# An RWKV-7 triangular inverse moved from two array quadrants to four

## The reference

```
S_t = S_{t-1} (diag(decay_t) - kk_t^T (kk_t * a_t)) + v_t^T k_t
o_t = S_t r_t
```

## Time and profile before

| | |
|---|---|
| median of 3 runs | 2339.93 us |
| the profiled execution | 2337.96 us |
| its span | 2336.3 us |
| TensorE busy (matmul) | 2150.9 us, 92% |
| VectorE busy | 912.5 us, 39% |
| ScalarE busy | 634.7 us, 27% |
| mean granted TensorE clock | 0.966 |

### The profile page before, as it was taken

How to read it: one execution, slowest core, us unless ns; L and a number is a source line. 1 busy time by engine, 2 the same in 40 slices (tenths; PEclk the granted TensorE clock), 3 DMA queues, 4 the chain that set the end, 5 groups by cost and what they waited for, 6 DMA issues and landing times. The chain is left out here.

```text
span 2336.3 us, 47109 instructions
## 1 busy us (share of the span) xinstructions
PE 2150.9 (92%) x20794; PEld 1409.6 (60%) x20794; DVE 912.5 (39%) x1765; ACT 634.7 (27%) x1433; POOL 319.8 (14%) x279
## 2 busy tenths in 40 slices
PE   7999999999999999997997999999898788489997
PEld 3577585675866857754554555556566555355664
DVE  3253462543634535323323313062321777522332
ACT  5321222223223223122214111132221566211111
POOL 0000020110201101020001032120010566101110
PEclk9999999999999999999999999999997999799998
DMA  7100010000100000007002022100002000556662
GB/s 255 30 20 11 10 41 19 29 21 10 31 26 27 17 19 30 21 15 281 1 27 104 27 85 76 54 10 9 28 27 73 1 1 1 201 172 225 209 194 92
DMA packets 52798, 147.84 MB, mean 63 GB/s; under 512 B 11459, under 2 KB 20995, under 8 KB 51316
## 3 DMA queue, kind: packets, MB, share of 16 engines
q1 hardware_dynamic: 42612, 103.97, 13.2%
q0 software_dynamic: 9984, 40.87, 4.9%
HBM read 123.58 MB, written 21.24 MB: 62 GB/s over the span
## 5 line engine op out<-in xcount | busy, mean ns | idle before, releaser
L755 PE MATMUL psum<-xT,rw_w 128*128 128x384 f32 (+1 forms) x1152 | 397.7, 484 | 2.8 <-PEq L169 2.8
L755 PEld LDWEIGHTS psum<-xT,rw_w 128*128 128x128 f32 x1152 | 206.1, 189 | 119.9 <-issue 9.4
L2020 PE MATMUL psum<-spare,xT 128*128 128x384 f32 (+1 forms) x432 | 142.2, 492 | 1.5 <-PEq L169 1.5
L2020 PE MATMUL psum<-kvq_w,xT 128*128 128x384 f32 (+1 forms) x432 | 140.6, 487 | 0.0
L1298 DVE SCALAR_TENSOR_TENSOR rwkv_xs<-psum,rwkv_pc,rwkv_xsc 128x64 f32<-128x64 f32 x90 | 25.5, 284 | 238.9 <-PE psum L974 238.9
L2020 PEld LDWEIGHTS psum<-spare,xT 128*128 128x128 f32 (+1 forms) x432 | 79.8, 186 | 62.3 <-issue 12.8
L2020 PEld LDWEIGHTS psum<-kvq_w,xT 128*128 128x128 f32 (+1 forms) x432 | 79.0, 184 | 61.3 <-issue 11.2
L723 POOL DMA_DIRECT2D out<-rwkv_s x6 | 5.7, 955 | 755.2 <-ACT rwkv_out_p L1124 755.2
L1103 ACT COPY rwkv_r_sb<-psum 128x64 f32<-128x64 f32 x96 | 20.4, 212 | 326.1 <-PE psum L956 295.1
L2422 PE MATMUL psum<-V,yT 128*128 128x512 f32 x192 | 103.3, 664 | 0.0
L2099 DVE TENSOR_REDUCE kvq_ss<-kvq_sq 128x6 f32<-128x384 f32 (+1 forms) x36 | 19.9, 552 | 200.6 <-ACT kvq_sq L2062 200.4
(11 more groups left out here) (437 smaller groups left out, 4042.6 us busy)
## 6 DMA issues: line engine op xcount, KB each, us to landing
xT<-in_cache_k SPq DMA_DIRECT2D x64, 384.0 KB, 3.5
samp_vp<-in_cache_v POOLq DMA_DIRECT2D x64, 384.0 KB, 4.4
rw_w<-in_w_in SPq DMA_DIRECT2D x28, 512.0 KB, 3.7
front_w<-in_mem_w_kv SPq DMA_DIRECT2D x2, 2048.0 KB, 14.1
x_rows<-in_x_p SPq DMA_DIRECT2D x8, 512.0 KB, 13.8
h<-in_x_p SPq DMA_DIRECT2D x8, 512.0 KB, 13.9
residual<-h POOLq DMA_DIRECT2D x8, 512.0 KB, 3.1
xT<-in_w_out SPq DMA_DIRECT2D x2, 1536.0 KB, 13.2
```

The costliest lines, as they stand in the source:

```text
L755: mm = pe.matmul(out, w[:, load % 2, k, :], xT[:, k, a:b], start=(k == 0), stop=(k == KC - 1))
L2020: mm = pe.matmul(bank[0:r, j % 6, 0:W], xT[:, k, n * P:n * P + r], w[i % 2][:, k, :], start=(k == 0), stop=(k == KC - 1))
```

## The change

Even chunks keep everything as before. For odd chunks the products `m`, the transposed inverse `ee` and the transposes are written to the other half of the partitions (`other(hh, n)`), so that they use the quadrants (rows 0:64, columns 64:128) and (rows 64:128, columns 0:64). Groups are now made of every second chunk: group 0 the chunks 0, 2, 4, 6, group 1 the chunks 1, 3, 5, 7, and so on. Two groups of one octet of chunks are issued together, chunk by chunk in turn, and waited for together (`TOGETHER`).

The core of the diff:

```diff
+        NOCT = GROUPS // 2
+        TOGETHER = [(0, 1), (2, 3), (GROUPS,)]
+        H2 = CH // 2
...
         def group(g):
-            return slice(4 * g, 4 * g + 4) if g < GROUPS else slice(NPC, NCHUNK)
+            return slice(8 * (g // 2) + g % 2, 8 * (g // 2) + 8, 2) if g < GROUPS else slice(NPC, NCHUNK)
+
+        def chunk_pairs(gs):
+            return [(g, u, range(NCHUNK)[group(g)][u]) for u in range(4 if gs[0] < GROUPS else 1) for g in gs]
+
+        def other(hh, n):
+            return half[(hh + n) % 2]
...
-            def first_inverse(p, g):
-                pe.wait_ge(e0_ready, NG * p + g + 1)
-                for u in range(4 if g < GROUPS else 1):
+            def first_inverse(p, o):
+                pe.wait_ge(e0_ready, NG * p + min(2 * o + 2, NG))
+                if o == NOCT:
...
+                else:
+                    for u in range(8):
+                        n = 8 * o + u
+                        for hh, d in enumerate(half):
+                            mm = turned(bank[d, 2 * o, u * CH:(u + 1) * CH], ee[d, n, :], d)
+                            if u % 2:
+                                mm = pe.matmul(bank[other(hh, n), 2 * o + 1, u // 2 * CH:(u // 2 + 1) * CH], ident[d, d], ee[d, n, :],
+                                               start=True, stop=True)
                 mm.then_inc(d0_turned, 1)
+
+            def block_products(p, lev, gs):
...
+                    pe.wait_ge(d_ready, NTURN * p + before(STEPS.index((lev, gs[-1]))) + 1)
+                for g, u, n in chunk_pairs(gs):
+                    for hh, d in enumerate(half):
+                        mm = pe.matmul(level_bank(g)[other(hh, n), u, :], am[d, n, 0, :], dd[d, n, :], start=True, stop=True)
+                    if u == 3 or g == GROUPS:
+                        mm.then_inc(m_mm, 1)
+
+            def block_updates(p, lev, gs):
+                last = STEPS.index((lev, gs[-1]))
+                pe.wait_ge(m_ready, NLEV * p + last + 1)
...
+                        if lev < LAST:
+                            mm = pe.matmul(level_bank(g)[d, u, :], ee[o, n, :], mm_[o, n, :], start=True, stop=True)
+                        else:
+                            mm = pe.matmul(level_bank(g)[o, u, H2:CH], mm_[o, n, :], ee[o, n, H2:CH], start=True, stop=True)
...
+            def block_turns(p, lev, gs):
+                last = STEPS.index((lev, gs[-1]))
+                pe.wait_ge(d_ready, NTURN * p + last + 1)
+                if last >= 3:
+                    pe.wait_ge(e_ready, NTURN * p + last - 2)
...
+                        mm = turned(turn_bank(4 + k % 3, g)[other(hh, n), u, :], dd[d, n, :], d)
...
                     decay_products(p, f)
-                    if f >= 3 and f % 2 == 1:
-                        first_inverse(p, f // 2 - 1)
-                first_inverse(p, GROUPS - 1)
-                first_inverse(p, GROUPS)
+                    if f == 4:
+                        first_inverse(p, 0)
+                first_inverse(p, 1)
+                first_inverse(p, NOCT)
...
-                        mm = pe.matmul(bank[d, 0, 0:HS], am[d, n, 2, :], v_tok[d, n, :], start=True, stop=(n == 0))
+                    for hh, d in enumerate(half):
+                        mm = pe.matmul(bank[other(hh, n), 0, 0:HS], am[d, n, 2, :], v_tok[d, n, :], start=True, stop=(n == 0))
...
-                for g in range(NG):
-                    act.wait_ge(d0_turned, NG * p + g + 1)
-                    nc.scalar.copy(dd[:, group(g), :], turn_bank(g, g)).then_inc(d0_ready, 1)
+                for o in range(NOCT):
+                    act.wait_ge(d0_turned, (NOCT + 1) * p + o + 1)
+                    nc.scalar.copy(dd[:, 8 * o:8 * o + 8, :].rearrange("p n t -> p (n t)"), bank[:, 2 * o, :])
+                    nc.scalar.copy(ee[:, group(2 * o + 1), :], turn_bank(2 * o + 1, 2 * o + 1)).then_inc(d0_ready, 1)
```

More of the change, by code:

```diff
@@ new lines, in block_updates @@
+            def block_updates(p, lev, gs):
+                last = STEPS.index((lev, gs[-1]))
+                pe.wait_ge(m_ready, NLEV * p + last + 1)
+                if lev >= 1:
+                    pe.wait_ge(e_ready, NTURN * p + before(last) + 1)
+                for g, u, n in chunk_pairs(gs):
+                    for hh, d in enumerate(half):
+                        o = other(hh, n)
+                        if lev < LAST:
+                            mm = pe.matmul(level_bank(g)[d, u, :], ee[o, n, :], mm_[o, n, :], start=True, stop=True)
+                        else:
+                            mm = pe.matmul(level_bank(g)[o, u, H2:CH], mm_[o, n, :], ee[o, n, H2:CH], start=True, stop=True)
+                    if u == 3 or g == GROUPS:
+                        mm.then_inc(dm_mm, 1)
@@ L890, in middle @@
+                    sets = [gs for gs in TOGETHER if (lev, gs[0]) in STEPS]
+                    for gs in sets:
+                        block_products(p, lev, gs)
+                    for gs in sets:
+                        block_updates(p, lev, gs)
+                    if lev < LAST:
+                        for gs in sets:
+                            block_turns(p, lev, gs)
                     if lev >= 2 and p >= 1:
@@ L950, in recurrence @@
                     x = xs[:, n % 2, :]
-                    for d in half:
-                        mm = pe.matmul(bank[d, 0, 0:HS], am[d, n, 2, :], v_tok[d, n, :], start=True, stop=(n == 0))
+                    for hh, d in enumerate(half):
+                        mm = pe.matmul(bank[other(hh, n), 0, 0:HS], am[d, n, 2, :], v_tok[d, n, :], start=True, stop=(n == 0))
                     if n >= 1:
                         pe.wait_ge(x_ready, NPC * p + n)
-                        for d in half:
-                            mm = pe.matmul(bank[d, 0, 0:HS], arT[d, p % 2, n, 0, :], x[d, :], start=False, stop=True)
+                        for hh, d in enumerate(half):
+                            mm = pe.matmul(bank[other(hh, n), 0, 0:HS], arT[d, p % 2, n, 0, :], x[d, :], start=False, stop=True)
                     mm.then_inc(r_mm, 1)
@@ L963, in recurrence @@
                     pe.wait_ge(r_ready, NPC * p + n + 1)
-                    for d in half:
-                        mm = pe.matmul(bank[d, 0, HS:2 * HS], ee[d, n, :], r_sb[d, :], start=True, stop=True)
+                    for hh, d in enumerate(half):
+                        o = other(hh, n)
+                        mm = pe.matmul(bank[d, 0, HS:2 * HS], ee[o, n, :], r_sb[o, :], start=True, stop=True)
                     mm.then_inc(sa_mm, 1)
@@ L1283, in _ @@
                         else:
-                            nc.vector.tensor_tensor(ee[:, group(g), :], level_bank(g), ee[:, group(g), :], ALU.add).then_inc(fin_ready, 1)
+                            nc.vector.tensor_tensor(ee[:, group(g), H2:CH], level_bank(g)[:, :, H2:CH], ee[:, group(g), H2:CH],
+                                                    ALU.add).then_inc(fin_ready, 1)
                     if lev >= 2 and p >= 1:
```

46 lines of the change are left out of this document (14 added, 32 removed).

## The result

| kernel | median us | runs, lowest to highest | profiled execution: us, span | mean granted clock |
|---|---|---|---|---|
| before | 2339.27 | 4, 2338.32 to 2340.98 | 2337.96, 2336.3 | 0.966 |
| after | 2363.11 | 4, 2358.86 to 2366.22 | 2358.86, 2357.2 | 0.954 |

The change makes the kernel slower: ratio 1.0088 with a 95% interval of 1.0070 to 1.0105. The forecast was 2321, faster. The profiled execution of after is the fastest of its four; it lies 20.9 us above the profiled one of before.

A forecast was written before the change was run, and what follows sets the result against it. TensorE was taken to bound the levels. Pair 0 gives -5.2 + 1.7 = -3.5, five pairs 5 x (-4.9 + 1.7) = -16, together -19.5: 2339.9 to 2320.4, say 2321 us; range 2307 to 2366.

The forecast's parts named there:

- What bounds the levels before: Levels: TensorE bounds them, busy 27.35 of 28.20 us in pair 0 at 29.1 ns a record; six pairs about 178 us.
- Can four quadrants run at once: Levels' products: all four quadrants run together, a record falling from 29.1 to 14.6 ns.
- signs of being wrong: Profile after: 68 records still take 1.98 us, the clock falls in the levels, or levels start no later than before.
- The walk of a level: Step-by-step timing at 14.6 ns: a level takes 4.73 us against 5.6; levels 5.2 us less in pair 0, 4.9 in others.
- The first inverses: Before the levels: TensorE waits for VectorE's second group, so levels start 1.7 us later in every pair.
- The recurrence: Recurrence after the levels: nothing gained, since L965 waits for ScalarE's copy; 0 taken, upper bound 5 us.
- A: Levels: nothing overlaps, or records come no closer than 28.5 ns; +6.0 us a pair, 2376, slower; chance 0.17.
- B: Levels: half the gain, 22 ns a record; +0.8 us a pair, 2345; chance 0.12.
- C: Levels: the clock falls as TensorE idles; 2329 with one such stretch a pair, 2380 throughout; chance 0.11.
- D: Before the levels: the 1.7 us delay does not arise because VectorE catches up; 2311; chance 0.04.

The follow-up runs named there:

- stream 1: Kernel before with an appended stage of 512 products without waits on the two diagonal quadrants, 64 moving columns; the stage took 31.8 us.
- experiment 2: Changed kernel with the first octet's first inverses moved from after decay product f = 4 to after f = 5; 2351.01 us, ratio to before 1.0053.
- Experiment 3: Changed kernel with every product kept on the diagonal quadrant of its head, all else of the change kept; 2373.75 us, ratio 1.0133.
- 4: Kernel before with levels 1 to 3 laid out so one 128x128 product transposes two chunks of both heads; 2329.43 us, ratio 0.9955.
- 5: Kernel of experiment 4 with the gated transposes of the pair before moved later, two parts to the end of the levels; 2324.56 us, ratio 0.9939.
- 7: Kernel of experiment 2 with three quarters of the transposes in levels 1 to 3 left out, inverses not computed rightly; 2329.9 us, ratio 0.9958.

## Why the prediction was wrong

- **What bounds the levels before:** half right. TensorE is busy 27.27 of 28.14 us, but its 29.1 ns a record is both the array's rate (stream 1, one row without a pause) and within 3% of the rate at which instructions come. A second limit stood right behind the first. Before the change it showed in pair 0's levels by a single wait, which the prediction did not read; in pair 4, whose levels took 31.35 us at the full clock where pairs 1, 2 and 5 took 29.8 to 30.0, by two:

```profile
PE psum L732 <- issue: 0.3, 1, 0.3
```
```profile
PE psum L732 <- issue: 0.5, 1, 0.5
PE psum L868 <- issue: 0.3, 1, 0.3
```

- **Can four quadrants run at once:** right in the short run, the failed step in the long one. "I take 14.6, since each half of it is in a row" held for bursts; every row that it rested on was shorter than 256 instructions, or slower than the supply. Over a level of 384 instructions the supply allows 5.4 us at 14.1 ns an instruction and 6.0 at the 4.0 us a packet of pair 0, where the walk gave 4.73. The levels of six pairs, forecast 29.7 us shorter, became 5.8 longer. None of the rivals and none of the signs of being wrong named the supply. By the 60 cycles a matmul of the Trainium skill ("TensorEngine Tiling (Array Packing)", section Instruction Overhead) nearly all of the gain would be missing, and it is; but 66 records follow each other at 14.6 ns, under the 25 of that rule, so this is not its mechanism.
- **The walk of a level:** its waits came where drawn, and somewhat shorter. Level 0, which has instructions in store, took 5.54 us where 5.17 were forecast (172.54 - 167.00). The excess over the five levels is 6.5 us: 4.4 of pauses put down to issue, about 0.9 because the last level's updates (L861) stay on their chunk's diagonal pair of tiles at 29 ns, 64 records in 2.06 us, which I had counted on four quadrants, and the rest, some 1.2 us, is not traced to single rows.
- **The first inverses:** right, 1.6 us a pair for 1.7, shown by experiment 2.
- **The recurrence:** right, 0.0.
- **Rivals.** A, that records come no closer than 28.5 ns, is not what happened. Experiment 3 makes that case, and its 2373.75 for 2376 is in part luck: in the profiled executions the first inverses cost 16.0 us more than before (forecast 15.6), the levels 12.7 (forecast 20), and 8.0 come behind the last levels, for which the sum had nothing. B's 2345 is the price of a mean of 22 ns a record; its mechanism was left blank, and the supply is such a one, only with pauses. C happened in part: the clock fell in the levels of four pairs, and the dearest of them took 2.6 us more than pair 2. D is refuted.
- **What stays open:** why the granted clock is lower behind the last levels, where the code is the same. The kernels of experiments 2 and 3 show longer times there too (1390.3 and 1392.3 us from the last recurrence to the end); those of 4, 5 and 7 do not (1384.5, 1384.7 and 1383.8), though 7 is the kernel of 2 with transposes left out. These are single profiled executions, and no run changes that alone. Nor is it shown what sets the start of a packet, and so why a cycle takes 4.0 to 4.5 us in the levels and 3.5 to 3.75 in a bare stream.

## What to carry to other kernels

Count TensorE's instructions, not only its array time: where a stretch asks for more than one instruction per 14 to 16 ns over more than 256 of them, more quadrants give bursts and pauses. Then the gain is in products that do more each (here one 128x128 transpose for four of 64x64, which is slower on the array and still made the kernel 0.4% faster, 0.6% with its waits put right). Look for idle time put down to issue at even distances of 256 instructions; a demand about as fast as the supply hides the limit almost wholly, as it did here behind waits of at most 0.8 us a pair.

## What was not expected of the hardware

- Instructions for TensorE come in packets of 256, one at a time: one per 3.47 to 3.75 us in a bare stream that waits for them, one per 3.98 to 4.50 in the levels, and in no trace of this case two starts closer than 3.23 us.
- Records on four quadrants do follow each other at 14.6 ns, 128 in 2.09 us with the modelled tail, for 64x64 weights and 64 columns; a record of 128 columns costs about twice as much (655 on four in 18.93 us, 28.9 ns).
- In one execution each, a stream that keeps TensorE busy without a gap was granted 0.50 on one quadrant and 0.51 on the two column halves of one row half, but 0.93 on two row halves (1.00 after the first 7 us) and 1.00 on the diagonal (after 3.6 us at 0.53): busy time alone did not decide the clock.
